# Joining the loads of the first four up slices of each expert: one of 4 MB in place of two of 2 MB

## What is computed

```
logits = xt @ router_w + router_b                     # 256 tokens, 32 experts
top_vals, top_idx = top_k(logits, 4); gates = softmax(top_vals)
...
def expert_block(args):
    e, xb = args
    hu = xb @ w_up[e] + b_up[e]                       # 1024 x 2048 weights, 8 MB
    g = minimum(hu[:, :1024], 7)
    lin = clip(hu[:, 1024:], -7, 7)
    glu = g * sigmoid(1.702 * g)
    return ((lin + 1.0) * glu) @ w_down[e] + b_down[e]   # 1024 x 1024 weights, 4 MB
...
y = segment_sum(y_rows * row_gate, row_tok)
```

## Time and profile before

| | |
|---|---|
| median of 3 runs | 2917.61 us (2914.72 to 2919.38) |
| profiled execution | 2916.23 us |
| its span, first to last instruction | 2914.6 us |
| TensorE busy | 2800.6 us, 96% of the span |
| VectorE, ScalarE busy | 1282.5 us (44%), 1000.3 us (34%) |
| DMA | 737.74 MB, mean 253 GB/s |
| loads of slices 0 to 5, 2 MB each | median 18.1 us from issue to landing |

### The profile page before, as it was taken

One profiled execution on the slowest core, in us unless ns is written; L12 is line 12 of the kernel. 1 busy time (PEld: TensorE's weight loads), 2 busy tenths in 40 slices (PEclk: granted clock), 3 DMA queues, 4 the chain that ended last, 5 costly groups with the idle time before them and its releaser, 6 DMA issues. The chain is left out here.

```text
span 2914.6 us, 42256 instructions
## 1 busy us (share of the span) xinstructions
PE 2800.6 (96%) x16961; PEld 1995.5 (68%) x16961; DVE 1282.5 (44%) x1713; ACT 1000.3 (34%) x1302; POOL 68.5 (2%) x133
## 2 busy tenths in 40 slices
PE   7979999999999999899899999999899999999998
PEld 4764444444444443588788988888787889889887
DVE  2652111111111111465773745655654874555655
ACT  2321111111111111354423554544544424463553
POOL 4010000000000000100000000100100000000000
PEclk9988999999999999999999999999999999999999
DMA  9487999999999999876334434563855345335552
GB/s 348 166 334 329 428 428 428 428 428 404 429 429 428 429 428 429 331 214 197 109 115 143 155 109 144 158 203 128 245 190 159 103 123 161 120 110 169 184 186 76
DMA packets 276128, 737.74 MB, mean 253 GB/s; under 512 B 11128, under 2 KB 231856, under 8 KB 245792
## 3 DMA queue, kind: packets, MB, share of 16 engines
q1 hardware_dynamic: 271152, 726.70, 66.9%
q0 software_dynamic: 4848, 9.25, 1.4%
HBM read 734.86 MB, written 1.05 MB: 252 GB/s over the span
## 5 line engine op out<-in xcount | busy, mean ns | idle before, releaser
L519 PE MATMUL ps<-arena,ring 128*128 128x256 f32 x2304 | 513.4, 383 | 3.0 <-DMA ring<-in_w_in 3.0
L1841 PE MATMUL ps<-u_both,w_upper 128*128 128x512 f32 x1408 | 499.8, 399 | 3.6 <-DVE u_both L1970 3.6
L519 PEld LDWEIGHTS ps<-arena,ring 128*128 128x128 f32 x2304 | 438.0, 192 | 65.2 <-DMA ring<-in_w_in 3.2
L1843 PE MATMUL ps<-u_both,w_lower 128*128 128x256 f32 x1408 | 394.9, 280 | 0.0
L1964 DVE TENSOR_TENSOR w_lower<-ring,w_upper 128x2048 fp32r<-128x2048 f32 x128 | 293.4, 2292 | 192.7 <-ACT w_upper L1917 192.7
L1566 PE MATMUL ps<-arena 128*64 128x512 f32 x1568 | 345.7, 597 | 0.0
L1841 PEld LDWEIGHTS ps<-u_both,w_upper 128*128 128x128 f32 x1408 | 264.5, 188 | 70.9 <-DVE u_both L1970 6.1
L1696 DVE TENSOR_SCALAR arena<-ps 128x512 f32<-128x512 f32 x34 | 23.5, 692 | 636.5 <-PE ps L1566 636.5
L1917 ACT ACTIVATE w_upper<-ring 128x2048 fp32r<-128x2048 f32 x128 | 244.4, 1909 | 77.8 <-PE ps L1843 77.7
L1843 PEld LDWEIGHTS ps<-u_both,w_lower 128*128 128x128 f32 x1408 | 265.8, 189 | 1.4
L1566 PEld LDWEIGHTS ps<-arena 128*64 128x64 f32 x1568 | 110.0, 137 | 218.5 <-issue 217.4
(11 more groups left out here) (590 smaller groups left out, 3534.1 us busy)
## 6 DMA issues: line engine op xcount, KB each, us to landing
arena<-in_exp_w_up SPq DMA_DIRECT2D x94, 2048.0 KB, 18.1
ring<-in_exp_w_down SPq DMA_DIRECT2D x68, 2048.0 KB, 15.8
ring<-in_w_in SPq DMA_DIRECT2D x75, 1024.0 KB, 5.8
ring<-in_exp_w_up SPq DMA_DIRECT2D x34, 2048.0 KB, 20.8
ring<-in_ffn_w_gate SPq DMA_DIRECT2D x44, 1024.0 KB, 5.4
ring<-in_ffn_w_up SPq DMA_DIRECT2D x44, 1024.0 KB, 5.4
ring<-in_ffn_w_down SPq DMA_DIRECT2D x44, 1024.0 KB, 4.8
ring<-in_ada_w SPq DMA_DIRECT2D x20, 1024.0 KB, 8.7
```

What stands on the lines that cost most here:

```text
L519: ins = nc.tensor.matmul(bank(b, 2, TOK)[:, m, :], w[:, k, m * P:(m + 1) * P], rhs[:, k, :], start=(k == 0 and (part is None or (part == 0 ...
L1841: nc.tensor.matmul(both, wh[:, k, c], U2[:, k, :, :].rearrange("p a b -> p (a b)"), start=(k == 0), stop=False, skip_group_check=True)
L1843: ins = nc.tensor.matmul(both[:, 0:TOK], wl[:, k, c], UH[:, k, :], start=False, stop=(k == KT - 1), skip_group_check=True)
```

## The change

`up_loads` issues slices 0 to 3 as one transfer of 4 MB, whose run per partition is 32 KB, into four neighbouring slots; its wait is for the fourth of the slots (`count + 4`). It raises `e_ready[0]` or `o_ready[0]`. Slices 4 and 5 are loaded as before (`k == 4`). TensorE waits for `e_ready[0]` or `o_ready[0]` ahead of each of the slices 0 to 3, and for the third semaphore ahead of 4 and 5; the second isn't used any more.

```diff
@@ -309,20 +309,24 @@
 
             def up_loads(count, e, odd, first=False):
 
-                for k in range(0, ESLOTS, 2):
+                for k in (0, 4):
                     if count is None:
                         sp.wait_ge(w_used, (T_WOUT1 + 3) // SLOTS * SLOTS + SLOTS + (T_WOUT1 + 3) % SLOTS + 1)
                         if k == 4:
                             sp.wait_ge(sem("router_step"), 1)
                     else:
-                        sp.wait_ge(e_used, count + k + 2 if first is False else ESLOTS)
+                        sp.wait_ge(e_used, ESLOTS if first else count + (ESLOTS if k else 4))
                     sp.sem_inc(sem("slots_taken"), 1)
                     if odd and k == 4:
                         for j in range(2):
                             sp.dma_start(oslot(k + j), up_pairs(e)[k // 2][:, j, :]).then_inc(o_ready[k // 2], 16)
                         continue
-                    dst, landed_at = (opair(k), o_ready[k // 2]) if odd else (epair(k), e_ready[k // 2])
-                    sp.dma_start(dst, up_pairs(e)[k // 2]).then_inc(landed_at, 16)
+                    at, landed_at = (8192, o_ready) if odd else (EAT, e_ready)
+                    if k == 0:
+                        src = up[e].rearrange("(p j) n -> p j n", j=KT)[:, 0:4, :]
+                        sp.dma_start(view(at, 4, 2048), src).then_inc(landed_at[0], 16)
+                    else:
+                        sp.dma_start(view(at + 2048 * k, 2, 2048), up_pairs(e)[k // 2]).then_inc(landed_at[2], 16)
 
             def late_loads(b, e):
 
@@ -1600,9 +1604,9 @@
                 for k in range(KT):
                     if k < ESLOTS:
                         if odd:
-                            pe.wait_ge(o_ready[k // 2], loads * (32 if k >= 4 else 16))
+                            pe.wait_ge(o_ready[k // 4 * 2], loads * (32 if k >= 4 else 16))
                         else:
-                            pe.wait_ge(e_ready[k // 2], loads * 16 + (32 if k < EARLY else 0))
+                            pe.wait_ge(e_ready[k // 4 * 2], loads * 16 + (32 if k < 4 else 0))
                         up_slice(oslot(k) if odd else eslot(k), k).then_inc(e_used, 1)
                     else:
                         T = T_MOE + k - ESLOTS
```

## The result

| | before | after |
|---|---|---|
| median | 2916.71 us (12 runs) | 2920.68 us (12 runs, 2917.97 to 2928.97) |
| ratio, interval | | 1.0018 (1.0010 to 1.0027) |
| profiled execution | 2916.23 us | 2923.95 us |
| its span | 2914.6 us | 2922.3 us |

A forecast was written before the change was run, and what follows sets the result against it. The DMA, slower than TensorE by 0.8 us a block, was taken to set the loop's end; 3.4 + 1.1 + 0.55 - 2.2 = +2.9 us on the 2917.61 us median gave 2920.5 us, range 2915.5 to 2926.0.

The forecast's parts named there:

- What bounds the loop: Experts' loop: DMA needs 29.4 us a block, TensorE 28.56; DMA standstills are paid at the end, at most 4.8 us recoverable.
- elsewhere it is full: Experts' loop: the DMA stands still or nearly so only at 225 to 237 us and 686 to 690 us.
- First restart: Loop's start, buffers full: first issue moves from 236.3 to 239.7 us, 4 MB land at 254.2 instead of 250.8; costs 3.4 us.
- rival c: Loop's start: the slow 9.6 us landing isn't met again, costing 1.4 in place of 3.4 us; 2918.5 us, chance 0.15.
- Some 2.7 us are needed: DMA queue at a load's issue: less than about 2.7 us left means a new standstill; more is enough.
- Second restart: Block 16, two buffer sets become one: issue at 698.9 us with 1.8 us of queue left; costs 1.1 us, bounds 0 to 3.1.
- Tail: Block 33: TensorE waits for all 4 MB before slice 0 and reaches slice 6 0.55 us later, paid once.
- Longer runs: Joined loads in 34 blocks: 128 packets fewer each, at 8 ns a packet, gain 2.2 us; bounds 0 to 4.8.
- rival (b): Joined loads: split again into 16 KB packets, or longer packets worth nothing; +5.0 us, 2922.7 us, chance 0.15.
- rival a: Loop: DMA gets faster per load, by saved fixed part or longer packets; 4.8 us come back, 2912.8 us, chance 0.07.
- The loop as a whole: Experts' loop: 3.4 + 1.1 + 0.55 - 2.2 = +2.9 us.
- The scatter of the clock behind the loop: 1213 to 1220 us, just behind the loop: low granted clock may fall otherwise by some 3 us; not in the sum.

The follow-up runs named there:

- second comparison: The changed kernel, unchanged, measured again on another occasion against 30 runs of the kernel before: 2918.20 us, ratio 1.0007 (0.9998 to 1.0016).
- the late issue alone: Kernel before, slices 0 and 1 issued only with 2 and 3, still separate 2 MB loads: 2924.48 us (1.0026), again 2921.09 us (1.0018).
- the one joined later: Changed kernel, but slices 0 to 3 come as two loads issued apart in blocks 2 to 5 and 17 to 20: 2917.16 us, ratio 0.9999.

## Why the prediction was right or wrong

The forecast of 2920.5 us stands against 2920.68. The agreement to 0.2 us is luck: the loop gave less than foretold (+1.6 against +2.9), time at the lower clock behind it, which stood in no term, added about 2 us, and the 2917.61 us it started from is 0.9 over the median of the 12 runs. The second comparison, +1.2 us, would have missed by 1.7.

**What bounds the loop**: right. The free period stayed at 28.56 us, the DMA's came down by what the rate gave, and joining everywhere but near the restarts showed that what the DMA doesn't lose in standstills comes off the end of the loop (917.0 us). But the count of the standstills was short by one: "elsewhere it is full" was read from long windows, and the one from 257.5 to 259.5 us doesn't show in them.

**First restart, 3.4 us**: mis-sized, and for a wrong reason. Measured up to the last load of that round it is 1.6 us. The easy restart (rival c) is what happened for the first load: 12.0 us for 4 MB. "Place, queue and neighbours are the same" was no reason; the 9.6 us of the earlier trace rows were not a property of the place, since over the traces with a load of 2 MB there it took 7.1 to 9.6 us, 7.7 in one that issued it at 236.3 as before does. And the standstill that was overlooked is one that the changed kernel doesn't have, which accounts for most of the 1.9 us that came back of the later start.

**"Some 2.7 us are needed"**: this step failed. Joined loads with 2.9 and 3.4 us of queue left landed 1.7 and 1.1 us late, and before itself stood still from 257.5 us although its load of 2 MB was issued at 257.2 with 3.6 us left up to the landing ahead (246.7 + 14.2 = 260.9). The step took the queue's end from a landing, and the landings trail the data by amounts that differ. The prediction had the next joined load of block 3 at "4.4 to 6.4 us, which is enough"; with 4.5 us it came 0.3 us late in after, so this held by a narrow margin. How much data must be queued, and whether 4 MB want more than 2 MB, isn't known.

**Second restart, 1.1 us**: right in kind and size as far as the trace goes (12.7 us against 12.5). The sum of both restarts is 3.4 us in the changed kernel (920.0 = 918.4 + x + 0.55 - 2.4) and 2.9 us measured by the late issue alone, where 4.5 were foretold. In after the two restarts are late by 1.6 and 1.3 us (11.0 us behind the load ahead, where a queued one takes 9.7), which are the 2.9; the joined loads of blocks 3 and 18, 0.3 and 0.1 us late, make up most of the rest.

**Tail, 0.55 us**: right, 0.6 in the trace of after, with TensorE's wait moved from slice 6 to slice 0 as told.

**Longer runs, -2.2 us**: right, -2.3 to -2.4, carried over from what 8 KB packets cost against 16 KB ones. The run wasn't split, so rival (b) is out. That the DMA saves a fixed part for each load (rival a) is out as well: a joined load in the queue takes 9.7 us and two single ones 9.8. The Trainium skill's page "DMA: Bandwidth & Descriptors", section "Anatomy of one DMA — SWDGE (gpsimd) path", gives about 2 us of fixed cost for each DMA, and gives it for DMAs that GpSimd issues. For these loads, which SP issues and which stand in a queue, the trace does not agree with the 2 us saved that the prediction drew from it: 0.08 us were saved.

**The loop as a whole**: +2.9 foretold, +1.6 measured.

**The scatter of the clock behind the loop** was named and left out of the sum, as "can't steer". That was the second failed step. It is not only scatter: executions with a low mean clock are more frequent in the changed kernel (7 of 23 against 9 of 120), and that accounts for about as much as the change in the loop. That the time stays within 0.2% was given 0.75, and so it came: 1.0018 in the one comparison, with an interval that reaches beyond, and 1.0007 in the other.

## What to carry to other kernels

Before two loads are joined, look up how much queue each has ahead of it at its issue, not only on average but at the places where buffers have just filled or their number changes; there, issue small ones, and join where the queue is long. Whether the DMA stands still is read from its rate in slices well under a microsecond: wide windows hide a standstill of 1 or 2 us, and landings trail the data. With the DMA as the bound a longer run per packet gives a little (0.08 us in a load of 4 MB here), once loads are queued; a load's fixed part is worth nothing. And a saving of 1 or 2 us ahead of an idle stretch of TensorE may be lost or doubled behind it: cut two traces at the same place of the program and compare part by part, and compare executions of the same mean granted clock, before a difference of 0.1 to 0.2% is put down to an edit.

## What the runs showed of the hardware that was not expected

- A load of 4 MB with runs of 32 KB lands 9.7 us after the one ahead of it if it is issued with 5.5 us or more left to the landing of that one. With 4.3 to 4.7 us left it was 9.7 to 10.0, with 3.4 us 10.8, with 2.9 us 11.4, and with 1.7 us 11.0, so less queue was not always worse.
- The DMA can stand still while a landing is 3 us away: in before its rate was nothing from 257.5 to 258 us, and the load ahead landed at 260.9.
- Eight transposes ahead of the loop, 0.8 us of work, raised the median by 7.6 us; twenty behind it, 2.4 us, by 5.3. With the lower clock of 1.2 GHz from 1668 to 1675 us the same code did 21 matmuls where it did 33 at 2.4 GHz.
- The same load at the same place took 9.6 us to land in the first trace of before, 9.5 us in the one joined later and 7.7 us in a third kernel; the loads behind it landed at 271.3, 270.9 and 271.2 all the same.
